# A hybrid attention backbone on one core: both maxima first, the second map turned ahead of the even slots, squares ahead of gains, and grouped probabilities scaled by VectorE

## What is computed

```python
def gqa_attend(q, k, v):
    s = jnp.einsum('bqkgd,btkd->bkgqt', q * ATTN_SCALE, k).astype(jnp.float32)
    p = jax.nn.softmax(s, axis=-1).astype(v.dtype)
    return jnp.einsum('bkgqt,btkd->bqkgd', p, v)

def diff_attend(q, k, v, lam):
    s = jnp.einsum('bqhmd,bthmd->bhmqt', q * ATTN_SCALE, k).astype(jnp.float32)
    p = jax.nn.softmax(s, axis=-1)
    w = (p[:, :, 0] - lam * p[:, :, 1]).astype(v.dtype)
    return jnp.einsum('bhqt,bthe->bqhe', w, v)
```

## Time and profile before

| what | value |
|---|---|
| median of 3 runs | 2398.95 us (2397.9 to 2400.64) |
| profiled execution, its own time | 2396.41 us |
| span of that execution | 2394.6 us |
| TensorE busy | 2312.2 us, 97% of the span |
| VectorE busy | 1374.8 us, 57% |
| ScalarE busy | 1022.3 us, 43% |
| GpSimd busy | 857.5 us, 36% |
| grouped heads, first layer | 90.7 to 272.5 us of the span |
| grouped heads, second layer | 1466 to 1609 us of the span |

### The profile page before, as it was taken

The page is one execution under the profiler, slowest core; times in us unless marked ns, Lnnn a source line. Parts: engine busy times, 40 slices in busy tenths (PEclk is TensorE's granted clock), DMA queues, the critical chain, the costliest instruction groups (busy, mean ns, idle before and its releaser), DMA issues.

```text
span 2394.6 us, 32835 instructions
## 1 busy us (share of the span) xinstructions
PE 2312.2 (97%) x12832; PEld 2081.0 (87%) x12832; DVE 1374.8 (57%) x2068; ACT 1022.3 (43%) x1991; POOL 857.5 (36%) x593
## 2 busy tenths in 40 slices
PE   7999999999999989999999998999989998999999
PEld 3888899999999989999999997778878877888887
DVE  5566677699966845554442446667888945111111
ACT  4566676652252342112212236666754354422222
POOL 2556311100034424353343336752220144544443
PEclk9999999999999999999999999999999999999999
DMA  6100111123224523433433321011113333333333
GB/s 254 45 22 30 36 43 36 32 84 94 66 75 133 176 66 122 134 111 127 128 120 119 104 95 53 31 41 41 50 35 99 103 97 107 97 98 96 97 97 97
DMA packets 134665, 208.96 MB, mean 87 GB/s; under 512 B 12528, under 2 KB 66032, under 8 KB 134384
## 3 DMA queue, kind: packets, MB, share of 16 engines
q1 hardware_dynamic: 134512, 206.86, 27.2%
HBM read 202.62 MB, written 4.19 MB: 86 GB/s over the span
## 4 chain that ended last, share of the span: by engine, by line
PE 75%; DVE 14%; ACT 5%; issue 3%; DMA 1%; POOL 1%; SPq 0%; DVEq 0%; ACTq 0%
PE acc L708 20%; PE acc L709 19%; PE acc L710 19%; DVE X L1827 5%; PE aux L709 3%; PE aux L708 3%; PE aux L710 3%; PE sco L907 2%; ACT M L1172 2%; DVE RB L1693 2%; PE aux L920 2%; DVE NM L1739 2%; PE acc L942 1%; DVE M L1693 1%; DVE WLO L1693 1%
## 5 line engine op out<-in xcount | busy, mean ns | idle before, releaser
L601 POOL TENSOR_TENSOR WLO<-STG,WHI 128x512 fp32r<-128x512 f32 (+2 forms) x500 | 694.8, 1411 | 1408.5 <-ACT WHI L1168 1244.4
L708 PE MATMUL acc<-H,WHI 128*128 128x384 f32 (+2 forms) x1976 | 712.0, 360 | 20.9 <-DVE H L1992 8.7
L710 PE MATMUL acc<-H,WLO 128*128 128x384 f32 (+2 forms) x1976 | 694.6, 351 | 0.0
L709 PE MATMUL acc<-H,WHI 128*128 128x384 f32 (+2 forms) x1976 | 694.1, 351 | 0.0
L1168 ACT ACTIVATE WHI<-STG 128x512 fp32r<-128x512 f32 (+2 forms) x616 | 330.5, 585 | 391.4 <-PE acc L710 352.4
L708 PEld LDWEIGHTS acc<-H,WHI 128*128 128x128 f32 x1976 | 373.2, 189 | 51.3 <-issue 18.4
L710 PEld LDWEIGHTS acc<-H,WLO 128*128 128x128 f32 x1976 | 372.9, 189 | 25.2
L709 PEld LDWEIGHTS acc<-H,WHI 128*128 128x128 f32 x1976 | 373.7, 189 | 24.0 <-issue 0.2
L708 PE MATMUL acc<-RB,WHI 128*128 128x384 f32 (+1 forms) x816 | 288.6, 354 | 3.2 <-DVE RB L1693 1.4
L710 PE MATMUL acc<-RB,WLO 128*128 128x384 f32 (+1 forms) x816 | 287.6, 352 | 0.0
L709 PE MATMUL acc<-RB,WHI 128*128 128x384 f32 (+1 forms) x816 | 287.5, 352 | 0.0
(11 more groups left out here) (160 smaller groups left out, 2854.3 us busy)
## 6 DMA issues: line engine op xcount, KB each, us to landing
STG<-in_w_fi SPq DMA_DIRECT2D x176, 256.0 KB, 2.7
M<-in_w_mod SPq DMA_DIRECT2D x56, 512.0 KB, 4.7
STG<-in_w_in SPq DMA_DIRECT2D x104, 256.0 KB, 2.6
STG<-in_w_gate SPq DMA_DIRECT2D x96, 256.0 KB, 2.7
STG<-in_w_fo SPq DMA_DIRECT2D x64, 256.0 KB, 2.7
STG<-in_w_br SPq DMA_DIRECT2D x96, 128.0 KB, 2.1
FIRST<-in_w_mod SPq DMA_DIRECT2D x8, 1024.0 KB, 20.1
SOONB<-in_w_mod SPq DMA_DIRECT2D x16, 512.0 KB, 3.9
```

Source lines behind the costliest of these rows:

```text
L601: nc.gpsimd.tensor_tensor(WLO[:, s, a:a + w], STG[:, g, a:a + w], WHI[:, s, a:a + w].bitcast(F32), ALU.subtract).then_inc(S("w_split"), 1)
L708: nc.tensor.matmul(dst, lh, rh, start=first, stop=False)
L709: nc.tensor.matmul(dst, lh, rl, start=False, stop=False)
L710: return nc.tensor.matmul(dst, ll, rh, start=False, stop=last)
```

## The change

It has four parts. `gqa_probs` on VectorE now scales both maps of a grouped item itself, after waiting for its own reciprocal, and `scale_probs` on GpSimd is gone. On VectorE, `maximum` 1 stands ahead of `turned_lo` of map 0, in all heads. On ScalarE, in grouped heads, the even slot comes after `grouped_lo` and `turned_hi` of map 1, except where that slot holds the sums' factors or the turned values. In `evac_norm` the square comes first with a semaphore of its own (`xsw`), on which `head_sums` now waits, and the scaled copy second; the bank comes free after the second as before.

```diff
+        def squared(l, what, j, n):
+            before = sum(len(ranges(k, w)) * (HEADS if not w else 5) for k in range(l) for w in (False, True))
+            q, k = len(ranges(l, False)), len(ranges(l, True))
+            done = before + j * q + (1 + max(0, j - 4)) * k if j else before
+            if what == "ks":
+                return done + k
+            return done + q + (k if j == 0 or j >= 4 else 0)
...
-            def scale_probs(g, k0):
-                n = TOK if k0 == 0 else CTX
-                for m in range(2):
-                    s = 2 * (g % 2) + m
-                    c.step("recip")
-                    pool.wait_ge(S("recip"), c.at("recip"))
-                    nc.gpsimd.tensor_scalar(PR[:, s, 0:n], PR[:, s, 0:n], RL[:, s:s + 1], None, ALU.mult).then_inc(S("pg"), 1)
...
             def head_sums(p, n, name, uses, kind="acc"):
-                wait_free(kind, *uses)
+                pe.wait_ge(S("xsw"), squared(name[0], name[2], name[1], n))
...
-                fn(XG[:, p, a:a + w], src, ACT.Identity, scale=V[:, gain:gain + 1], bias=EC[:, 2:3], sem="xgw")
-                fn(XS[:, p, a:a + w], src, ACT.Square, sem=f"{kind}_free{b}")
+                fn(XS[:, p, a:a + w], src, ACT.Square, sem="xsw")
+                fn(XG[:, p, a:a + w], src, ACT.Identity, scale=V[:, gain:gain + 1], bias=EC[:, 2:3], sem=f"{kind}_free{b}")
...
-                    slot(j + 1, 2 * i, j < 4)
+                    sums = j >= 4 or 2 * i in [last_slots(l, j + 1).get(t, -2) + 1 for t in "qkv"]
+                    if sums:
+                        slot(j + 1, 2 * i, j < 4)
                     if g and grouped_pair(items[g - 1]):
                         grouped_lo(l, g - 1, items[g - 1][0], items[g - 1][2], 1)
                     if j < 4:
                         turned_hi((l, g, 1), PTS[1], P * (i % 2), k0)
+                        if not sums:
+                            slot(j + 1, 2 * i, True)
...
             def gqa_probs(g, k0):
+                n = TOK if k0 == 0 else CTX
                 for m in range(2):
                     s = 2 * (g % 2) + m
                     dve.wait_ge(S("exp" if m else "exp0"), c.at("sc0"))
-                    nc.vector.reciprocal(RL[:, s:s + 1], L[:, s:s + 1]).then_inc(S("recip"), 1)
-                    c.step("recip")
+                    own("recip", nc.vector.reciprocal(RL[:, s:s + 1], L[:, s:s + 1]))
+                    nc.vector.tensor_scalar(PR[:, s, 0:n], PR[:, s, 0:n], RL[:, s:s + 1], None, ALU.mult).then_inc(S("pg"), 1)
...
                     if after:
                         maximum(0, g + 1, after[3])
-                    turned_lo((l, g, 0), PTS[0], P * (i % 2), k0)
                     if after:
                         maximum(1, g + 1, after[3])
+                    turned_lo((l, g, 0), PTS[0], P * (i % 2), k0)
```

More of the change, by code:

```diff
@@ L617, in attention @@
                     split(KC * P)
-                scale_probs(0, 0)
                 for g, (j, i, q, k0) in enumerate(items):
-                    if g + 1 < len(items) and items[g + 1][0] < 4:
-                        scale_probs(g + 1, items[g + 1][3])
                     for s in (2 * i, 2 * i + 1):
@@ L624, in attention @@
                             split(tile_width[c.at("tile")])
-                c.step("recip", 2 * sum(item[0] >= 4 for item in items))
             nc.gpsimd.memset(EC[:, 0:1], EPS).then_inc(S("ec"), 1)
```

## The result

The changed kernel takes 2403.41 us in the median (2400.51 to 2406.54, 20 runs), the kernel before 2397.48 us on the same chips (2393.57 to 2400.64, 20 runs): ratio 1.0027, 95% interval 1.0021 to 1.0033. The profiled execution has a span of 2401.0 us against 2394.6.

The account below looks back on a forecast made before the run. TensorE was taken as the bound. Terms 12.5 (late slot) + 2.0 + 2.2 (maxima, grouped heads) + 0 - 1.0 (GpSimd waits) = 15.7 us slower, giving 2414 us; own range 2406 to 2421, full range 2398 to 2426.

Parts of the forecast that it names:

- all else: Forecast terms besides the late even slot: +2.0 and +2.2 us grouped heads, 0 differential heads, 0 squares, -1.0 GpSimd waits.
- Second map turned before the slot: ScalarE's late even slot in grouped heads: evacuations lie bare behind the weighing and TensorE waits; +12.5 us.
- Order of the maxima: VectorE: late turned_lo and longer chain cost +2.2 and +2.0 us in the two layers' grouped heads; differential heads sum 0.
- Scaling moved to VectorE: Grouped items: 45 us of new VectorE work, 5.7 us of TensorE waits on GpSimd go; -1.0 us left as gain.
- Rival (3): VectorE becomes the bound as scalings wait for GpSimd's splits: 12 us on top, 2427 us; chance 0.14.
- Squares first: Square and scaled copy swapped on ScalarE: head sums wait for VectorE's bank, not for the squares; 0 us.
- Rival (1): Second map's earlier turning ends waits at head sums and next scores: gain 16 us at most, half gives 2391; chance 0.14.
- Rival (2): Evacuation waits merge with TensorE waits already standing there, each part pays for the other: 2400 us; chance 0.12.

Follow-up runs that it names:

- no_bare: The changed kernel, but ScalarE's even slot comes late only where it holds no evacuation; 2386.78 us, ratio 0.9961 to the kernel before.
- only_max: The kernel before with only the second maximum put ahead of turned_lo of the first map; 2382.59 us against 2397.05, ratio 0.9936.
- max_held: As only_max, but ScalarE's second exponential also waits for the first map's turned_lo; 2399.02 us against 2395.59 for the kernel before, ratio 1.0014.
- only_slots: The kernel before with only ScalarE's even slot moved behind the second turned_hi; 2406.46 us against 2397.05, ratio 1.0037.

## Why the prediction was right and wrong

**Forecast and result.** 15.7 us were forecast on a profiled execution, the spans differ by 6.4. The forecast is the sum of two terms, 12.5 for the late slot and 3.2 for all else. no_bare splits the result in the same way: 2401.0 - 2384.4 = 16.6 us for the late slot's evacuations, 2384.4 - 2394.6 = -10.2 us for all else. So the forecast was 4.1 us too low on the one and 13.4 too high on the other, and the direction was right because the part that was said to decide did decide. The first miss made up for 4.1 us of the second in the total, and that is luck.

**Second map turned before the slot: right, size 16.6 for 12.5.** Item by item, changed kernel less no_bare:

| place | forecast, us | measured, us |
|---|---|---|
| first layer, first head, third and fourth item | 0.3 | 0.94 - 0.74 |
| fifth item, heads one to four | 1.3, 1.6, 1.6, 2.1 | 1.3, 2.0, 3.1, 3.6 |
| first item, fourth head, first layer | 1.8 | 1.6 |
| first item, fourth head, second layer | 2.2 | 2.2 |
| third item, fourth head, second layer | 1.6 | 1.7 |

The chains of instructions gave five of these within 0.2 us and one within 0.4. The two that missed by 1.5 us are those with a stretch at half clock behind the wait. A matmul of a 384-column chunk starts every 0.32 us there and every 0.18 at full clock (nine in 1.67 us in no_bare, from 200.90 on), so 3.4 us at half clock do the work of 1.9: 1.5 us lost, and that is the miss. The remaining 0.9 us are spread over items where the forecast had nothing.

**Order of the maxima: the step that failed.** The prediction said that the exponential starts 0.7 us sooner and then let that gain in, for the grouped heads, only as a reduction of VectorE's longer chain ("Its 1.4 us longer work, less what the earlier exponential saves, leaves +0.7 us per head"), and it priced the late `turned_lo` at 0.8 us for every odd item. Measured with this part alone: -14.5 us. In only_max the steps are -2.8 us over the first layer's grouped heads, -8.3 over the second's and -3.4 over the second layer's differential heads. The prediction had +2.2, +2.0 (both with the scaling's chain in them) and -0.9. TensorE does wait for the late `turned_lo`, but an item as a whole is longer than before in six places only, by 0.5 to 1.1 us. What was left out is that ScalarE stands still for the second maximum, and VectorE behind it for the exponential (fifteen waits in the sixteen items of the second layer's stage), and that TensorE's large waits hang on these chains. These waits in that stage, in only_max (first three) and in max_held:

```profile
PE aux L920 <- DVE RB L1693: 3.6, 6, 0.9
PE sco L907 <- DVE RB L1693: 2.0, 3, 0.7
PE aux L885 <- DVE XP L1693: 1.9, 3, 0.6
...
PE sco L907 <- DVE RB L1696: 5.5, 3, 1.8
PE aux L885 <- DVE XP L1696: 4.1, 3, 1.4
```

The head sums' 5.8 us became 1.9 and the scores' 4.4 became 2.0. With the exponential held and all else as in only_max they are 4.1 and 5.5 again, and 16.4 us of span come back (2397.2 and 2380.8). The prediction also took the idle time of TensorE in the two grouped stages for "nearly all that can be won": 3.7 us of what only_max wins is busy time that the clock gives back, and 3.4 us lie in the second layer's differential heads.

**Scaling moved to VectorE: right alone, half right in the sum.** The durations were right: the wide scalings take 0.62 us and the narrow ones 0.35 in the trace. The forecast was -1.0 for the GpSimd waits and +0.7 per head for the chain; alone the part is worth 0 (1.0003), on the new maxima it costs 6.6 us. The steps that give this are the third items of the second layer's heads, where it costs 1.1 to 1.7 us, about the 1.4 us of longer work that were argued.

**Rival (3), VectorE delayed by splits: excluded.** Of the 80 scalings of the changed kernel four overlap a split of GpSimd. The group of them (count, min/median/max ns), and then, from the timeline, the one place with long ones:

```profile
L1768 DVE TENSOR_SCALAR M<-M,RL x80: 352/620/1307, 93.0 to 1616.3; 128x768 f32<-128x768 f32 x64, 128x256 f32<-128x256 f32 x16
```

```profile
272.03 2.56 POOL L610 TENSOR_TENSOR WLO<-STG,WHI 128x512 fp32r<-128x512 f32 x2 [14.38 <-ACT WHI L1164]
...
272.16 1.31 DVE L1768 TENSOR_SCALAR M<-M,RL 128x256 f32<-128x256 f32 x1
...
273.57 1.18 DVE L1768 TENSOR_SCALAR M<-M,RL 128x256 f32<-128x256 f32 x1
```

Two narrow ones take 1.31 and 1.18 us, each beside one of the two splits that take 2.56 us together, in place of 0.35, two wide ones 0.72 and 0.70 in place of 0.62: 2.0 us of VectorE's time in all, against the 23 that the rival needed. The mechanism is there, and the trace agrees with what the Trainium skill says (SBUF — State Buffer, section Who interferes with whom) of instructions of the two engines that exclude each other; it was the number of meetings that decided.

**Squares first: right, 0.** **Rival (1), faster:** all parts but the bare evacuations gained 10.2 us of its 16 at most, and the waits that it named did shrink, but by the order of the maxima. Of the second map's earlier turning, only_slots shows gains of 1.3 to 1.6 us in four items of the second layer, against evacuations that were not hidden. **Rival (2), a wash:** the total came nearer to it than to the forecast (+6 where it had +1), but not by its reason, since neither wait covered the other: two effects of opposite sign, each over 10 us, stand in different items.

## What to carry to other kernels

When an instruction is moved on one engine, follow also what the *other* engines wait for in the idle time of that engine, not only the waits of the bottleneck: here 12 us of VectorE's waits for an exponential in one stage, none of them a wait of TensorE, stood at the head of both chains that TensorE waited on. Put the instruction that releases another engine before the one that only frees a buffer, then look item by item where the buffer was wanted first, and undo it there: the five exceptions gave about 4 us on top of 15. An evacuation of an accumulator must not be placed behind work that waits for the very matmuls that it is to overlap; before it is moved, ask for each slot whether the bank is the next one that TensorE opens.

## What the runs showed of the hardware

A TensorE wait can cost about twice its length. Behind waits of 1.77 us at 213.61 and at 271.49 the kernel after has matmuls at a granted clock of 0.50, which costs 1.5 us more each, and no_bare has neither these waits nor these stretches. The three such stretches of the kernel before in the second layer's grouped heads go with the maxima alone, and the kernel after has three again there (0.50 from 1501.00 to 1504.00, from 1535.20 to 1538.20 and from 1569.20 to 1572.20). But not each wait of that length does it: in the kernel after, the clock is 1.00 behind the second head's wait of the same 1.77 us and the one of 1.75 us in the fourth head's first item.

```profile
170.79 0.44 PE L704 MATMUL acc<-H,WHI 128*128 128x384 f32 x1 [1.77 <-ACT U L1168]
```

```profile
171.00:175.00 4.00, 4.00 (x29) 3.49 (x29) 3.14 (x9) 0.48 (x2) 0.00 (x0) 1.00 0.00 0
231.00:235.00 4.00, 3.98 (x28) 3.48 (x29) 0.37 (x1) 0.00 (x0) 0.00 (x0) 1.00 0.00 0
```

What tells the two kinds apart I did not try, so a forecast of such a wait has these two prices.

Two maxima of 768 columns that follow each other directly take 1.82 us together (1536.69, above), and 0.96 + 0.95 apart, so side by side they gave 0.1 us and not more.
